# Split-weight buffers at three different address remainders

## The reference

```
for i in range(2):
    u = x * (1.0 + sc1) + sh1
    y = gla_mixer(u, ...) if i == 0 else chunk_attention(u, ...)
    x = layer_norm(ALPHA * x + (1.0 + g1) * y, ...)
    u = x * (1.0 + sc2) + sh2
    x = layer_norm(ALPHA * x + (1.0 + g2) * (square(relu(u @ w1)) @ w2), ...)
h = x + hybrid_mixer(rmsnorm(x), ...)
h = h + conv_ffn(rmsnorm(h), ...)      # (silu(a) * b) @ w_down, a and b from a width-3 convolution of h @ w_up
return rmsnorm(h)
```

## Time and profile before

| | |
|---|---|
| median of 3 runs | 1059.03 us (1057.78 to 1060.43) |
| profiled execution, own time | 1062.04 us |
| its span, first to last instruction | 1060.3 us |
| mean granted TensorE clock | 0.987 of full speed |
| TensorE busy | 1014.4 us, 96% of the span |
| VectorE busy | 802.0 us, 76% |
| ScalarE busy | 507.4 us, 48% |
| moved by DMA | 227.94 MB, mean 215 GB/s |

### The profile page before, as it was taken

The page is one execution under the profiler, slowest core; times in us unless marked ns, Lnnn a source line. Parts: engine busy times, 40 slices in busy tenths (PEclk is TensorE's granted clock), DMA queues, the critical chain, the costliest instruction groups (busy, mean ns, idle before and its releaser), DMA issues.

```text
span 1060.3 us, 16558 instructions
## 1 busy us (share of the span) xinstructions
PE 1014.4 (96%) x6776; PEld 910.6 (86%) x6776; DVE 802.0 (76%) x1109; ACT 507.4 (48%) x683; POOL 68.4 (6%) x143
## 2 busy tenths in 40 slices
PE   6999998999999999998999999799999989999996
PEld 6987777998999798887998999598988979999995
DVE  3499798999988877658787566857885858777776
ACT  2393425334343656625433433544456555555553
POOL 2101210000000111000100000100000000000000
PEclk9999998999999999998999999899999999999998
DMA  9968866799998474434864554263343445565551
GB/s 344 382 219 323 288 238 222 297 349 342 343 337 298 139 265 139 169 118 141 337 247 171 189 201 153 103 213 132 129 158 121 155 138 184 188 203 187 179 187 72
DMA packets 35051, 227.94 MB, mean 215 GB/s; under 512 B 4096, under 2 KB 4224, under 8 KB 10144
## 3 DMA queue, kind: packets, MB, share of 16 engines
q1 hardware_dynamic: 25232, 167.01, 45.0%
q0 software_dynamic: 9744, 59.87, 15.3%
HBM read 225.82 MB, written 1.05 MB: 214 GB/s over the span
## 4 chain that ended last, share of the span: by engine, by line
PE 84%; DVE 7%; issue 3%; ACT 3%; DMA 2%; POOL 1%; POOLq 0%; DVEq 0%; ACTq 0%
PE ps L440 76%; DMA ada_raw<-ada 2%; ACT weight_hi L1079 1%; PE ps L649 1%; DVE weight_lo L1500 1%; PE ps L660 1%; PE ps L853 1%; PE ps L961 1%; DVE att_s L1992 1%; PE ps L666 1%; PE ps L843 0%; DVE dev L1690 0%; DVE dev L1683 0%; ACT att_s L1299 0%; PE ps L842 0%
## 5 line engine op out<-in xcount | busy, mean ns | idle before, releaser
L1500 DVE TENSOR_TENSOR weight_lo<-weight_raw,weight_hi 128x2048 fp32r<-128x2048 f32 (+2 forms) x192 | 361.7, 1888 | 89.9 <-ACT weight_hi L1079 89.8
L1079 ACT ACTIVATE weight_hi<-weight_raw 128x2048 fp32r<-128x2048 f32 (+2 forms) x168 | 299.2, 1786 | 69.2 <-PE ps L440 59.9
L440 PE MATMUL ps<-act_hi,weight_hi 128*128 128x256 f32 x1336 | 327.1, 286 | 4.7 <-DVE act_lo L1625 3.6
L440 PE MATMUL ps<-act_lo,weight_hi 128*128 128x256 f32 x1336 | 322.3, 282 | 0.0
L440 PEld LDWEIGHTS ps<-act_hi,weight_hi 128*128 128x128 f32 x1336 | 254.7, 191 | 13.4 <-issue 10.9
L440 PEld LDWEIGHTS ps<-act_lo,weight_hi 128*128 128x128 f32 x1336 | 254.7, 191 | 3.1 <-issue 1.0
L440 PE MATMUL ps<-act_hi,weight_lo 128*128 128x256 f32 x1336 | 177.9, 280 | 0.1
L440 PEld LDWEIGHTS ps<-act_hi,weight_lo 128*128 128x128 f32 x1336 | 164.9, 188 | 0.5 <-DVE weight_lo L1500 0.3
L440 PE MATMUL ps<-weight_hi,mlp_hi 128*128 128x512 f32 x256 | 100.5, 393 | 0.0
L440 PE MATMUL ps<-weight_hi,mlp_lo 128*128 128x512 f32 x256 | 99.6, 389 | 0.0
L1261 ACT ACTIVATE mlp_hi<-mlp_relu 128x512 fp32r<-128x512 f32 x32 | 20.3, 633 | 158.1 <-DVE mlp_relu L1936 151.1
(11 more groups left out here) (321 smaller groups left out, 1341.8 us busy)
## 6 DMA issues: line engine op xcount, KB each, us to landing
weight_raw<-weights SPq DMA_DIRECT2D x144, 1024.0 KB, 5.1
ada_raw<-ada POOLq DMA_DIRECT2D x48, 1024.0 KB, 7.6
weight_raw<-weights SPq DMA_DIRECT2D x23, 512.0 KB, 3.6
row_g<-ln_rows POOLq DMA_DIRECT2D x4, 512.0 KB, 4.6
row_b<-ln_rows POOLq DMA_DIRECT2D x4, 512.0 KB, 5.7
att_bias<-rel_bias POOLq DMA_DIRECT2D x16, 128.0 KB, 3.4
square<-ada_rows POOLq DMA_DIRECT2D x3, 512.0 KB, 3.9
dev<-x_in SPq DMA_DIRECT2D x1, 1024.0 KB, 5.4
```

The costliest lines, as they stand in the source:

```text
L440: return e.matmul(o, a, b, start=start, stop=False, skip_group_check=True)
L1079: e.activation(weight_hi[h][:, 0:size], weight_raw[r][:, 0:size], ACT.Copy).then_inc(hi_full[h], 1)
L1500: ins = e.tensor_tensor(weight_lo[h][:, c], weight_raw[r][:, c], weight_hi[h][:, c].bitcast(F32), ALU.subtract)
```

## The change

Ahead of each of the three pairs `weight_hi[i]`, `weight_lo[i]` there is a filler, so that the pair has its own remainder: 192 for buffer 0, 32 for buffer 1 and 128 for buffer 2. The order in memory changes with it: before, the three hi tiles came first and then the three lo tiles; after, each hi tile is followed by its lo tile.

```diff
 LINE, STAYING, MOVING = 256, 128, 64
+
+WEIGHTS = (192, 32, 128)
 INDEX_W = 2 * HD + IDX_H
...
         to_phase("weights", nc.sbuf_base, STAYING)
         weight_raw = [sb(f"weight_raw{i}", [P, CW]) for i in range(N_RAW)]
-        weight_hi = [sb(f"weight_hi{i}", [P, CW], F32R) for i in range(N_SPLIT)]
-        weight_lo = [sb(f"weight_lo{i}", [P, CW], F32R) for i in range(N_SPLIT)]
+        weight_hi, weight_lo = [], []
+        for i in range(N_SPLIT):
+            to_phase(f"weight{i}", nc.sbuf_base, WEIGHTS[i])
+            weight_hi.append(sb(f"weight_hi{i}", [P, CW], F32R))
+            weight_lo.append(sb(f"weight_lo{i}", [P, CW], F32R))
         ada_raw = [sb(f"ada_raw{i}", [P, CW]) for i in range(N_ADA_RING)]
```

## The result

The changed kernel takes 1065.95 us in the median of five runs (1063.46 to 1066.25), the kernel before 1059.77 in five (1057.78 to 1061.46). The ratio is 1.0052, with a 95% interval of 1.0037 to 1.0067. I had forecast 1052.4, faster.

A forecast was written before the change was run, and what follows sets the result against it. TensorE was taken as the bound, by the distance between matmul starts. Up chunks -8.3 us and row chunks +1.7 us gave -6.6 us, from a median of 1059.0 to 1052.4 us; range 1047.5 to 1063.5.

The forecast's parts named there:

- What bounds the kernel: MLPs and convolutional FFN: TensorE always busy, so time is the number of matmuls times the distance between their starts.
- The up chunks: MLPs and FFN: 39 slow chunks on buffers 0 and 1 go from 117.7 to 113.3 ns a matmul, -8.3 us.
- outer bound (+4.1 us): Up and projection chunks: two thirds of the 29 fast chunks could fall to the slow pace, +4.1 us.
- The row chunks: MLP, FFN and output projection rows: 816 matmuls lose distance 0, from 226.7 to 228.8 ns, +1.7 us.
- Act-stationary rows: Row chunks with act tiles loaded: 288 matmuls go to distances -128 and +32; bounds -0.6 to +1.3 us, 0 taken.
- Buffer 2: Up chunks on buffer 2: remainder stays 128, distance +64, so their pace stays as before.
- a case with all three buffers fast: Up chunks: slow pace handed on, so buffer 2's 19 chunks gain too; -12.4 + 1.7, 1048.3 us, chance 0.10.
- The last of my signs of being wrong: Profile after: prediction is wrong if the pace label changes with the place in the program and not with the buffer.
- ScalarE and VectorE: First MLP's splits on moved tiles: no change, 1902 and 2286 ns for a full chunk; not on the path.
- The slower case: Row chunks on buffers 0 and 1 fall to 233.2 ns, ups stay slow: +5.3 us, 1064.3 us, chance 0.24.
- the first rival: Matmul paces throughout come from the order of work alone, so nothing happens: 1059.0 us, chance 0.20.
- The rule of the Trainium skill: TensorE's two SBUF read ports never wait for anyone, so remainders change nothing and the sum is 0.

The follow-up runs named there:

- dummy: The kernel before with one extra small matmul (32 columns, result unused) ahead of every projection chunk, no address changed; ratio 1.0013.
- split1: The kernel before with the last lo matmul of every row chunk done as two halves of 256 columns; 1053.41 us, ratio 0.9942.
- only0: The changed kernel with only buffer 0 leaving remainder 128 (192, 128, 128); ratio 1.0041 against the kernel before.
- same128: The kernel before with act and mixer tiles at remainder 128 instead of 64, so both operands at distance 0; ratio 1.0115.
- only1: The changed kernel with only buffer 1 leaving remainder 128 (128, 32, 128); ratio 1.0055 against the kernel before.
- after_dummy: The changed kernel with one extra small matmul (32 columns, result unused) ahead of every projection chunk; 1076.56 us in a single execution.

## Why the prediction was wrong

- **What bounds the kernel** was right: distances between matmuls on one line. No other engine moved, and the +6.8 us of the three forms account for the 6.2 us between the medians.
- **The up chunks** are the step that failed. I took 113.3 ns for the 39 changed chunks, -8.3 us, "because a slow pace that holds without one exception [...] is a fixed relation of two address streams, and the change breaks just this relation". The form as a whole came out at +1.5 us, 9.8 us away from this term; that is most of the miss (-6.6 us forecast, +6.2 measured). The runs showed two errors in it. The slow pace was not fixed by the addresses: in dummy and split1 the same pair ran at 113.3. And breaking the relation of addresses does not lead to the fast pace: the two new distances have their own, 118.6 and 116.7, both worse than the fast one, while the old distance +64 was the only one that had the fast pace. So in the MLPs and the FFN the change made buffer 0's ups 0.8 ns slower and buffer 1's 1.1 ns faster, and in the mixer and attention stages it turned chunks that had been at 1.98 us into ones at 2.02 to 2.06. I had this loss only as an outer bound (+4.1 us). The count in it was a little off too: 25 chunks with sixteen lo products in a row were at the fast pace, not 29.
- **The row chunks** had the right mechanism and the wrong size: +1.7 us predicted, +4.5 measured, 5.5 ns for each of the 816 moved matmuls where I took 2.1. At the distance -64 I was near (228.8 taken; 229.4 in the MLPs, which is 228.8 behind a start-up of a few matmuls); at +96, for which I had no row, I took the same, and it is 234.0.
- **Act-stationary rows**: 0 taken, +0.8 us measured, inside the bounds I gave.
- **Buffer 2**: predicted unchanged. Its ups went to 113.7 in the MLPs and stayed at 117.8 in the FFN, where the row chunks between them are half as long. This pace is handed on, as only0 shows by taking it back; I had this as a case with all three buffers fast. The last of my signs of being wrong, a pace that changes with the place in the program, is what happened here.
- **ScalarE and VectorE**: right, no change.
- **The rivals.** The slower case named the loss of the rows' distance 0 as its mechanism and 1064.3 us as its time, near the measured 1065.95. The mechanism is two thirds of what was measured (+4.5 of +6.8 us), but its size came from buffer 1 at +96 and not from -64 falling to 233.2, and the rest from the lost fast chunks; that the time came out so near is partly luck. The evidence for it, that distance 0 is the best for rows wherever it is used, was the better argument. Of the first rival (the order of work sets the pace) the half that I wrote down as a memory of something other than the address turned out true, and it should have told me that the slow ups could not be taken as a property of their addresses.
- **The rule of the Trainium skill** (SBUF — State Buffer, section Who interferes with whom), that TensorE's two read ports are independent and wait for no one, doesn't hold here if it is read as a statement on pace: remainders alone made 119.9 of 117.8 ns (same128) and 234.0 of 226.7 (only1).
- **What stays open.** Why a matmul starts later at one distance of remainders than at another no run shows. Nor does one show the rule by which a pace is handed on: a 24-matmul row chunk at 234 leads buffer 2 to the fast pace in the changed kernel's MLPs but not in only1's, and with the 12-matmul rows of the FFN it is the other way round. In only1 the distances add up to about 4.0 us where the medians are 4.9 us apart, and in only0 to 5.6 where they are 3.7 apart; these differences are unexplained.

## What to carry to other kernels

Where one engine is the bound and its instructions run end to end, measure the distance between starts by shape and by what stands before: two paces of one shape at one pair of addresses are a sign that the pace is handed on, and then a small change of pattern at the boundary (here one matmul in two halves, 0.6%) is worth trying before any tile is moved. If tiles are moved, count what the fast places lose as well as what the slow ones may win: a pair of remainders that is seen to run at the best pace anywhere is an asset, and none of the five others tried here for the up form reached it. Test remainders for each form of product by itself, since the best distance of one form (0 for the rows) was the worst of the other, as far as tried.

## What the runs showed of the hardware that I had not expected

- The distance between matmuls depends on the difference of the remainders, by 256 bytes, of the loaded and the moving tile's addresses, and did not change when both moved by 64 (shift64: equal to 0.1 ns). That 256 bytes is the right period is how this kernel counts; no run varied it. At full granted clock the spread is 113.3 to 119.9 ns for 256 columns and 226.7 to 234.0 for 512.
- One pair of addresses can run at two steady paces, 113.3 and 117.8 ns at +64 (116.7 and 117.8 at -32), and keeps the one it falls into for the whole chunk of 48. A single odd matmul ahead, or a last matmul in two halves, changes which (dummy, after_dummy, split1).
- The best distance depends on the form: 0 bytes for 512 moving columns (226.7 against 228.8 at -64, 233.3 at +64 and -32, and 234.0 at +96), 64 for 256 moving columns (113.3 or 117.8 against 119.9 at 0).
